# Recurrent block's gate products from high and low float32r parts, with GpSimd copying the inputs' high parts

## The reference, cut to what matters

```python
u = h @ w_in + b_in                      # 1024 -> 2048 columns
x_br, y_br = u[..., :1024], gelu(u[..., 1024:])
xc = conv_b + sum(xp[:, tap:tap + S] * conv_w[tap] for tap in range(4))
xb = xc.reshape(B, S, 8, 128)
r  = sigmoid(einsum('bsnc,nce->bsne', xb, w_ga) + b_ga)
ig = sigmoid(einsum('bsnc,nce->bsne', xb, w_gx) + b_gx)
log_a = -8 * r * softplus(-a_param)
a, b_seq = exp(log_a), sqrt(-expm1(2 * log_a)) * (ig * xc)
hs = scan of h[t] = a[t] * h[t-1] + b_seq[t]
out = (hs * y_br) @ w_o + b_o
```

## Time and profile before

| what | value |
|---|---|
| runs | 975.89, 977.11, 977.18 us; median 977.11 |
| span of the profiled execution | 975.9 us |
| time of the profiled execution | not listed apart; the lowest of the runs (975.89) fits its span |
| TensorE busy | 968.3 us |
| DVE, ACT, GpSimd busy | 680.5, 588.6, 66.2 us |
| chain that ended last | TensorE 99% |

### The profile page before, as it was taken

How to read it: one execution, slowest core, us unless ns; L and a number is a source line. 1 busy time by engine, 2 the same in 40 slices (tenths; PEclk the granted TensorE clock), 3 DMA queues, 4 the chain that set the end, 5 groups by cost and what they waited for, 6 DMA issues and landing times.

```text
span 975.9 us, 13399 instructions
## 1 busy us (share of the span) xinstructions
PE 968.3 (99%) x5146; PEld 826.0 (85%) x5146; DVE 680.5 (70%) x1161; ACT 588.6 (60%) x1042; POOL 66.2 (7%) x80
## 2 busy tenths in 40 slices
PE   8999999999999999999999999999999999999997
PEld 6887788888888898888888888888888888988886
DVE  5877786666568789666665588778767554877564
ACT  6777755454457897645454467547876555684443
POOL 1322110000000242000000000000011000000000
PEclk9999999999999999999999999999999999999999
DMA  9753545655455445555655556445543544335551
GB/s 368 296 194 134 184 173 186 224 176 211 174 196 185 146 165 192 182 187 184 226 178 207 177 198 250 173 175 188 198 165 105 193 148 170 132 133 209 177 189 44
DMA packets 27119, 180.33 MB, mean 185 GB/s; under 512 B 2992, under 2 KB 3888, under 8 KB 6320
## 3 DMA queue, kind: packets, MB, share of 16 engines
q1 hardware_dynamic: 26336, 176.98, 50.7%
q0 software_dynamic: 288, 2.10, 0.6%
q10 hardware_dynamic: 432, 0.39, 0.1%
HBM read 178.41 MB, written 1.05 MB: 184 GB/s over the span
## 4 chain that ended last, share of the span: by engine, by line
PE 99%; DMA 1%; DVE 0%; ACT 0%; SPq 0%; issue 0%; DVEq 0%
PE bank L338 25%; PE bank L293 16%; PE bank L295 16%; PE bank L294 16%; PE bank L346 13%; PE bank L308 1%; PE bank L468 1%; PE bank L484 1%; PE bank L589 1%; PE bank L518 1%; PE bank L309 1%; DMA front<-in_front 1%; PE bank L529 1%; PE bank L404 0%; PE bank L399 0%; PE bank L400 0%
## 5 line engine op out<-in xcount | busy, mean ns | idle before, releaser
L1349 DVE TENSOR_TENSOR lo<-raw,hi 128x1024 fp32r<-128x1024 f32 x318 | 375.9, 1229 | 20.1 <-ACT hi L822 19.9
L822 ACT ACTIVATE hi<-raw 128x1024 fp32r<-128x1024 f32 x318 | 320.3, 1050 | 100.1 <-PE bank L295 98.2
L338 PE MATMUL bank<-X,hi 128*128 128x512 f32 x1016 | 266.3, 394 | 0.0
L338 PEld LDWEIGHTS bank<-X,hi 128*128 128x128 f32 x1016 | 185.0, 189 | 32.8
L346 PEld LDWEIGHTS bank<-X,lo 128*128 128x128 f32 x1016 | 138.5, 190 | 10.1
L346 PE MATMUL bank<-X,lo 128*128 128x256 f32 x1016 | 141.6, 282 | 0.0
L853 ACT ACTIVATE bt<-bank 128x256 f32<-128x256 f32 x135 | 51.0, 380 | 141.5 <-PE bank L338 133.1
L1363 DVE TENSOR_TENSOR zr<-bank,bt 128x256 f32<-128x256 f32 x64 | 27.2, 424 | 108.9 <-ACT bt L853 108.9
L293 PE MATMUL bank<-hi,zh 128*128 128x512 f32 x256 | 100.0, 390 | 0.0
L295 PE MATMUL bank<-hi,zl 128*128 128x512 f32 x256 | 99.8, 390 | 0.0
L294 PE MATMUL bank<-lo,zh 128*128 128x512 f32 x256 | 99.6, 389 | 0.0
(11 more groups left out here) (345 smaller groups left out, 1420.5 us busy)
## 6 DMA issues: line engine op xcount, KB each, us to landing
raw<-in_w SPq DMA_DIRECT2D x64, 1024.0 KB, 4.7
raw<-in_rin SPq DMA_DIRECT2D x8, 1024.0 KB, 4.8
raw<-in_wk SPq DMA_DIRECT2D x4, 1024.0 KB, 10.3
raw<-in_wq SPq DMA_DIRECT2D x4, 1024.0 KB, 8.3
raw<-in_wo SPq DMA_DIRECT2D x4, 1024.0 KB, 4.7
raw<-in_mk SPq DMA_DIRECT2D x4, 1024.0 KB, 4.8
raw<-in_mv SPq DMA_DIRECT2D x4, 1024.0 KB, 4.8
raw<-in_rout SPq DMA_DIRECT2D x4, 1024.0 KB, 4.6
```

Source lines behind the costliest of these rows:

```text
L338: return PE.matmul(bank[b][:, :], wh[:, c:c + P], x[:, k_, :, :].rearrange("p a b -> p (a b)"), start=k_ == 0, stop=k_ == NC - 1, skip_gro ...
L822: ACTE.activation(hi[u_ % HIS][:, c], raw[u_ % RAW][:, c], ACT.Copy).then_inc(hi_cut, 1)
L1349: DVE.tensor_tensor(lo[u_ % RAW][:, c], raw[u_ % RAW][:, c], hi[u_ % HIS][:, c].bitcast(F32), ALU.subtract).then_inc(lo_cut, 1)
```

## The change

The gate weights are cut into float32r parts `gwh` (ACT, two copies) and `gwl` (DVE, two subtractions), one half behind round 8 and one behind round 10 of the first MLP. Each chunk of the convolved input is cut too: GpSimd copies the high part `xch`, DVE subtracts for the low part `xcl`, each with room for four chunks. DVE makes the low parts of a pair behind the half tiles that it cuts at the head of the next `to_x`, those of the last pair behind three of the four half tiles that follow. `gates(n)` waits for `xc_low` of its chunk and makes each product with `mm3`, three float32r matmuls. GpSimd's copies stand a pair ahead of its multiplications; from chunk 4 on a copy waits until TensorE and DVE are done with the chunk four before. Places in memory move: `gw` to slot 8, its parts to slots 14 and 4, the inputs' parts to slot 11.

```diff
@@ -116,6 +116,7 @@
     exp_made, p_made, o_high = sem("exp_made"), sem("p_made"), sem("o_high")
     z_made, z_high, z_low = sem("z_made"), sem("z_high"), sem("z_low")
     tap_made, xc_made, t_made = sem("tap_made"), sem("xc_made"), sem("t_made")
+    gw_high, gw_low, xc_high, xc_low = sem("gw_high"), sem("gw_low"), sem("xc_high"), sem("xc_low")
     gi_made, a_made, aa_made, mass_made, root_made, drive_made = (
         sem("gi_made"), sem("a_made"), sem("aa_made"), sem("mass_made"), sem("root_made"), sem("drive_made"))
     y_made, hs_gated, g_high, g_low = sem("y_made"), sem("hs_gated"), sem("g_high"), sem("g_low")
@@ -199,7 +200,9 @@
     q, k, v = slot("q", 5), slot("k", 6), slot("v", 7, [2, D])
     oh, ol = slot("oh", 10, dt=F32R), slot("ol", 11, dt=F32R)
     T = slot("T", 8, [16, 256])
-    gw = slot("gw", 14, [2, NC, P])
+    gw = slot("gw", 8, [2, NC, P])
+    gwh, gwl = slot("gwh", 14, [2, NC, P], F32R), slot("gwl", 4, [2, NC, P], F32R)
+    xch, xcl = slot("xch", 11, [4, S], F32R), slot("xcl", 11, [4, S], F32R, off=4096)
     both = [place(f"both{i}", o_tmp + 2048 + 1536 * i, [384]) for i in range(2)]
     mk, mv = slot("mk", 3), slot("mv", 4, [2, D])
     bo = slot("bo", 6, [D], off=4096)
@@ -582,11 +585,11 @@
         half("mk", 2, 1, M2, 5)
 
         def gates(n):
-            p.wait_ge(xc_made, n + 1)
-            p.wait_ge(gatew_in, 16)
+            p.wait_ge(xc_low, n + 1)
+            p.wait_ge(gw_low, 2)
             for m, b in ((0, 6 * (1 - n % 2)), (1, 7 - 6 * (n % 2))):
                 done = fill(("gate", n, m), b)
-                PE.matmul(bank[b][:, 0:S], gw[:, m, n, :], xc[:, n, :], start=True, stop=True).then_inc(done, 1)
+                mm3(bank[b][:, 0:S], gwh[:, m, n, :], gwl[:, m, n, :], xch[:, n % 4, :], xcl[:, n % 4, :], True, True).then_inc(done, 1)
 
         cols_as_ready("rin", 0, X2, (7, 6), "mix1")
         for i in range(1, 4):
@@ -997,6 +1000,10 @@
                         ACTE.activation(zh[i % 3][:, j, :], zf[c % 4][:, :], ACT.Copy).then_inc(z_high, 1)
                 if i > 0:
                     at_tile(f"w2_{n}", i - 1)
+                if n == 0 and i in (8, 10):
+                    m_ = i // 2 - 4
+                    a.wait_ge(gatew_in, 16)
+                    ACTE.activation(gwh[:, m_, :, :], gw[:, m_, :, :], ACT.Copy).then_inc(gw_high, 1)
 
         mlp(0, 0)
         ACTE.preload_act_table_set(LOGS)
@@ -1528,6 +1535,10 @@
                                           ALU.subtract).then_inc(z_low, 1)
                 if i > 0:
                     at_tile(f"w2_{n}", i - 1)
+                if n == 0 and i in (8, 10):
+                    m_ = i // 2 - 4
+                    d.wait_ge(gw_high, m_ + 1)
+                    DVE.tensor_tensor(gwl[:, m_, :, :], gw[:, m_, :, :], gwh[:, m_, :, :].bitcast(F32), ALU.subtract).then_inc(gw_low, 1)
 
         mlp(0, 0, "wo")
         lo_to(2 * (T_OF["mk", 1] + 2))
@@ -1550,8 +1561,15 @@
         step(DVE.memset(xbr[:, :, 0:3], 0.0))
         own()
 
+        def xc_lows(i):
+            for n in (2 * i, 2 * i + 1):
+                d.wait_ge(xc_high, n + 1)
+                DVE.tensor_tensor(xcl[:, n % 4, :], xc[:, n, :], xch[:, n % 4, :].bitcast(F32), ALU.subtract).then_inc(xc_low, 1)
+
         def to_x(i):
             lo_to(2 * (T_OF["rin", i] + 2))
+            if i:
+                xc_lows(i - 1)
             for n in (2 * i, 2 * i + 1):
                 joined(xbr[:, n, 3:XW], "rin", n)
             for w in range(1, 4):
@@ -1570,6 +1588,8 @@
 
         for i in range(4):
             to_x(i)
+        lo_to(2 * (T_OF["rin", 4] + 2) + 1)
+        xc_lows(3)
         lo_to(2 * (T_OF["rin", 4] + HIS))
         for n in range(0, NC, 2):
             d.wait_ge(aa_made, n + 2)
@@ -2008,9 +2028,22 @@
         POOL.dma_start(gw[:, :, :, :], A["gatew"]).then_inc(gatew_in, 16)
         for j in range(2):
             by_rows(mk, "mk", j, "mem", 2, mk_scaled)
-        for n in range(NC):
-            g.wait_ge(*free["gate", n, 1])
-            POOL.tensor_tensor(ig[:, n, :], ig[:, n, :], xc[:, n, :], ALU.mult).then_inc(gi_made, 1)
+
+        def xc_highs(i):
+            for n in (2 * i, 2 * i + 1):
+                g.wait_ge(xc_made, n + 1)
+                if n >= 4:
+                    g.wait_ge(*full["gate", n - 4, 1])
+                    g.wait_ge(xc_low, n - 3)
+                POOL.tensor_copy(xch[:, n % 4, :], xc[:, n, :]).then_inc(xc_high, 1)
+
+        xc_highs(0)
+        for i in range(4):
+            if i < 3:
+                xc_highs(i + 1)
+            for n in (2 * i, 2 * i + 1):
+                g.wait_ge(*free["gate", n, 1])
+                POOL.tensor_tensor(ig[:, n, :], ig[:, n, :], xc[:, n, :], ALU.mult).then_inc(gi_made, 1)
         for j in range(2, 6):
             by_rows(mk, "mk", j, "mem", 2, mk_scaled)
         for n in range(NC):
```

## The result

The changed kernel takes 982.88 us (median of 5 runs, 982.1 to 983.51) where the kernel before takes 977.18 in runs on the same chip. The ratio is 1.0058, with a 95% interval of 1.0046 to 1.007: 5.7 us slower. Forecast were 983.9 us, 980.2 to 988.5.

A forecast was written before the change was run, and what follows sets the result against it. TensorE, without idle time, was taken as the bound. Late low parts, handed on between pairs, delay the gate blocks by 1.8, 2.0, 3.2 and finally 6.8 us, products' gain included: 977.1 + 6.8 = 983.9 us, range 980.2 to 988.5.

The forecast's parts named there:

- The bound and the missing cover: TensorE is busy 958.0 of 958.0 us mid-kernel, so a wait put on it there cannot be made good later.
- The slack at `rout`: Before `rout`, the first gated low part is there at 374.7 us and TensorE wants it at 376.65.
- Products: In the recurrent block's gate blocks, twelve float32r matmuls cost 1.44 us instead of 1.72; four blocks gain 1.1 us.
- The gain of 1.1 is inside these: The gate blocks' delays of 1.8, 2.0, 3.2 and 6.8 us were said to include the products' gain already.
- Weights' cuts: In the first MLP, two ACT copies and two DVE subtractions fall into idle time and cost nothing.
- The hand-on of delays: In the recurrent block each pair's delay passes to the next: gate blocks late by 1.8, 2.0, 3.2 and 6.8 us.
- stages three and four: The third and fourth chunk pairs of the recurrent block, whose gate blocks were forecast 3.2 and 6.8 us late.
- c: Time of one GpSimd copy of 128x256 in the convolution, taken as 0.5 us; 2c, 1.0 us, charged per pair.
- The clock: Rival: TensorE's clock falls in the longest wait, at the fourth gate block, losing 1.8 us more: 985.7 us; chance 0.15.
- My wait of 3.8 us: TensorE's forecast standing time before the fourth gate block, the longest of about 2.1, 0.5, 1.5 and 3.8 us.
- Only the order costs: Rival: gaps take up every delay from pair to pair, the last pair alone pays +2.4 us, 979.5; chance 0.06.
- Not slower: Rival: the gate blocks' results come in time and only the products count, -1.1 us, 976.0; chance 0.05.

The follow-up runs named there:

- `late_first`: The changed kernel with DVE's subtractions ahead of its weight cuts and GpSimd's eight multiplies behind its eight copies: 978.59 us, 1.0016 against the kernel before.
- `f32_products`: The changed kernel with all its parts and waits, but the gate products are the single f32 ones of before: 981.86 us, 1.0053 against the kernel before.
- `dve_copy_first`: The changed kernel with subtractions ahead of the weight cuts and the high-part copies on DVE itself instead of GpSimd: 979.4 us, 1.0023 against the kernel before.
- `late_mult`: The changed kernel with only GpSimd's eight multiplies moved behind its eight copies: 981.97 us, 1.0049 against the kernel before.
- `no_low`: The changed kernel without DVE's low-part subtractions; products wait for GpSimd's copy alone and take the high part twice: 981.44 us, 1.0049 against the kernel before.
- `last_first`: The changed kernel with only the last pair's DVE subtractions moved ahead of the weight cuts: 978.75 us, 1.0015 against the kernel before.
- `lows_first`: The changed kernel with all four pairs of DVE subtractions moved ahead of the weight cuts: 979.39 us, 1.0019 against the kernel before.

## Why the prediction was right

**The bound and the missing cover.** Right. TensorE had no idle time in which to win the waits back: the 5.5 us lost in the stage are still there at `rout`, and in the total. The slack at `rout` was read too large, as `late_first` shows, but in the changed kernel the products and the chain to `rout` are late together, so that it cost nothing.

**Products.** Right for the products alone: 1.1 us forecast, 0.9 measured. "The gain of 1.1 is inside these" is not right: a block's end was reckoned from DVE's first result, so only the last block's 0.28 us is in the 6.8, and `f32_products` shows that no more of it counts.

**Weights' cuts.** Right: nothing.

**The hand-on of delays.** Right in kind, too large in size. The ends of the four gate blocks lie 1.5, 1.4, 1.7 and 5.3 us behind those of before (next tile at 328.06, 335.28, 342.87 and 352.62, less 0.24, against 326.33, 333.66, 340.98 and 347.04). Forecast were 1.8, 2.0, 3.2 and 6.8. The last block's first result was forecast for 352.4 and came at about 349.6. Two terms were mis-sized:
- *Taps in stages three and four.* I carried the 3.56 us that six taps took beside GpSimd's multiplies in the earlier trace rows over to the new kernel. There the multiplies stand behind the copies and meet the subtractions, and the taps take 2.56. That gives a microsecond back in each of the two stages. DVE's additions are 2.0 us late in the third handing-on (341.92 less 0.24 against 339.64), not 3.4.
- *The copies.* c was taken as 0.5 and is 0.40, and the charge of 2c per pair was the wrong shape: the copies lie behind the cuts, DVE waits 0.29 us for the first, and the second overlaps its subtraction. With the multiplies beside it, the pair of subtractions then takes 1.46 us, where 0.75 was taken and the first stage has 0.92. From the last cut to the next additions it is 1.2 us in the first stage and 1.8 in the others, against 1.75 charged: here the sum was nearly right for another reason.

**The clock.** I gave this its own case with 0.15 and 985.7 us. It happened in the profiled execution: clock 0.57 in the 4 us behind the last wait, the products 0.21 us apart (350.27 to 352.41) instead of 0.12. The block took 2.72 us for 1.44, and the first products of the tile behind it some 0.1 more: about 1.4 us, where the start's rows had given 1.8. All five runs of the changed kernel have a mean clock of 0.997 or 0.998. So the time of 982.9 is waits of about 4.3 us net (an estimate: 5.7 less 1.4) and a clock of 1.4, not 6.8 of waits. That the total came within 1.0 us of the forecast is partly luck: waits taken 2.5 us too large and a fall of the clock that the central case left out nearly cancel. Without the fall the time would have been about 981.5, still within the range. My wait of 3.8 us for the last block was 2.55, and even that brought the clock down. The Trainium skill (TensorE: Matmul & The Clock Gate, Part 1) has TensorE return to half clock after idling; the traces here agree. The shortest wait behind which it fell is 1.82 us, in `dve_copy_first` (TensorE, then a stretch of it with a granted clock of 0.59):

```profile
347.57 0.39 PE L296 MATMUL bank<-xch,gwh 128*128 128x256 f32 x1 [1.82 <-DVE xcl L1573]
...
348.00:351.00 3.00, 3.00 (x18) 0.59 0.00 0
```

They also show that it isn't certain: behind 2.17 us in `late_mult`, 2.42 in `f32_products` and 2.81 in `no_low` the profiled executions kept the full clock.

**Rivals.** "Only the order costs" fell: its condition, that delays from pair to pair are absorbed, was met only in part (with every delay absorbed, `last_first` would have lost nothing against before, and lost 1.4 us). "Not slower" needed the last pair's first result by 345.3; it came at about 349.6. The rest of the range held.

That the first three waits and the last one have different causes was not in the prediction: the last comes mainly from the three cuts ahead of it. The first comes from the two cuts and the copy that they keep out (0.9 us of it even in `no_low`). That the delay then isn't worked off, and that reordering the first three pairs gave nothing, comes from the load of a DVE that takes longer per pair than TensorE.

## What to carry to other kernels

Where one engine is busy without a gap, price a new dependence by the queue positions of every link in its chain, in each round of the loop and not in the first alone: work behind other work in an in-order queue is as late as that work. Then compare the cycle of the helping engine with that of the bound one; DVE was busy 70% of the span, but in this stage it took 7.60 us for a pair where TensorE needed 7.05. Move first what stands behind the longest run of other work: the last pair alone gave back 4.1 of the 5.7 us. Where the parts can't come earlier, let the bound engine do something else first: that gave back 1.0 us more.

## What the runs showed of the hardware

GpSimd's copy, given out under DVE's last tap, was kept out for a whole run of two-input DVE instructions: 2.85 us behind two cuts, 3.99 behind three, and 5.13 behind four in `no_low`. Where DVE had no cut next, as in `lows_first`, the same copy took 0.40 to 0.59. The Trainium skill (SBUF — State Buffer, "Who interferes with whom") has such an instruction and a GpSimd one that reads SBUF exclude each other for the whole instruction; here the copy was kept out for up to four in a row. Yet other GpSimd instructions got in between two cuts, as all of the eight multiplies in `late_first` did, in turn. What decides between the two behaviours stays open: no run varies the moment of arrival alone.

The fall of the clock behind waits of 1.8 to 2.8 us, in some executions of one kernel and not in others, spreads its times: `no_low` lies between 979.73 and 983.35 us, `last_first`, whose longest wait in the stage is 1.5 us, between 978.13 and 979.15.
